# Down weights asked for in blocks of 64 partitions by four successive rows, with the hidden units renumbered to match

## The chip, the cores and the metric

The kernel runs on one core of a Trainium2 chip. The metric is the device time of one execution in microseconds (us). Before the change the median of three runs is 2054.45 us (2053.09 to 2056.13). The time of the changed kernel is compared with that.

## The reference, cut to what matters

The reference is a chain of two blocks of two layers each, in float32, on 256 tokens of width 1024. The change touches only the second layer of the first block: a mixture of 8 experts, of which each token uses 2. What is computed there is

```
def swiglu(x, w_gate_up, w_down):
    g, u = jnp.split(x @ w_gate_up, 2, axis=-1)
    return (jax.nn.silu(g) * u) @ w_down

out = sum over e of combine[:, e:e+1] * swiglu(xf, w_gate_up[e], w_down[e])
# w_gate_up[e]: 1024 x 7168 (gate 3584 columns, up 3584 columns);  w_down[e]: 3584 x 1024
```

Per expert that is 29.36 MB of gate and up weights and 14.68 MB of down weights, 352 MB for all eight, and each byte is read once from HBM. The hidden width of 3584 may be numbered in any order as long as gate, up and the rows of down agree.

## The kernel before

The kernel gathers for each expert at most 96 of its tokens (`CAPACITY`), as three groups of 32 (`TRIPLE`, `GROUP`), and runs the experts one after the other. If more tokens chose an expert, a second path (`r == "f"`) takes the rest; the change leaves it alone.

**Up and gate.** For the products with the gate weights (`EG`) and the up weights (`EU`) the 32 gathered tokens of a group are the stationary operand (128 rows of the contraction by 32 columns), and the weights stream past as the moving operand. TensorE's 128 columns are used as four quarters (`QUADS`): quarter z multiplies the same 32 tokens by another quarter of the weight columns and writes partitions 32z to 32z+31 of a PSUM bank. The 3584 hidden columns are done in two parts, `half` 0 of 2048 columns and `half` 1 of 1536. So one instruction has 512 moving columns in half 0 and 384 in half 1 (`UNITS_OF`). In the profile these are the groups of L1376; each float32 product stands there as two records.

Which weight columns quarter z takes is set in `up_tile` at line 1371: a row of 2048 weights is seen as (t z j) with j of 128, so quarter z takes four pieces of 128 columns (three in half 1), 512 columns apart.

**Turning.** The gate goes through SiLU on ScalarE and is multiplied by up on VectorE (L3124). The product `gated` has tokens on partitions; the down product needs hidden units there. VectorE turns it in blocks of 32 by 32 (`dve.transpose`, L3128). One block takes 32 columns of `gated` that lie 4 apart. After it, partition p and block (t, c) hold hidden unit 512t + 4p + c of the half.

**Down.** In `down`, 32 columns of the turned tensor are stationary and 256 columns of a down weight row are moving, again with four quarters (L1408). Tile k holds 512 rows of the down weights as 128 partitions by 4 rows; partition p has rows 4p to 4p+3 of the 512, which is what the turned order asks for.

**Loads.** All weights come through `ring`, five slots of 2 MiB. SyncE's instruction stream (SP) issues two transfers per tile (`load`, L924), each after waiting for the slot to be given back by TensorE (L921). `sources` says which bytes they take. For a gate or up tile each of the two takes 128 partitions by one row piece of 8 KB (half 0) or 6 KB (half 1). For a down tile the first takes rows 0 and 1 of each partition's four, and the second rows 2 and 3: 128 partitions by 8 KB each. TensorE waits for a whole tile (both transfers, a count of 32) in `weights`. The order of tiles per expert is: gate half 0 (4 tiles), up half 0 (4), gate half 1 (4), up half 1 (4), down (7). TensorE does them in that order.

The sequence of instructions around the change is written out by hand, and no planner decides anything here. Loads run ahead of TensorE by as much as the five slots allow.

Of the kernel before, what the change touches and what calls it, by code (L numbers as in the profile page):

```python
# [17 lines left out]
P = 128  # L18
SEQ, D = 256, 1024
TB = SEQ // P  # L20
KC = D // P
LAYERS = 2
EPS = 1e-6
WIDE = 512
# [9 lines left out]
D_FF, EXPERTS, D_EXP = 2816, 8, 3584  # L34
# [365 lines left out]
def kernel_program(nc, t):  # L400
# [30 lines left out]
    with ctx:  # L431
# [58 lines left out]
        def shaped(v, *shape):  # L490
            if len(shape) == 1:
                return v
            names = "abcd"[:len(shape)]
            return v.rearrange(f"p ({' '.join(names)}) -> p {' '.join(names)}",
                               **{k: s for k, s in zip(names[1:], shape[1:])})
# [357 lines left out]
        def tile_view(name, k, n):  # L853
            r = tiles_f if name in tiles_f.place else tiles
            return ring[:, r.slot(name), 0:k * n].rearrange("p (k n) -> p k n", n=n)

        def parts(src, k):

            v = src.rearrange("(k p) n -> p k n", p=P)
            return [(0, k // 2, v[:, 0:k // 2, :]), (k // 2, k, v[:, k // 2:k, :])]  # L860
# [35 lines left out]
        def sources(name, e):  # L896

            kind = name[0]
            if kind in ("EG", "EU") and name[1] == "m":
                a, n = HALF * name[2] + D_EXP * (kind == "EU"), QUADS * UNITS_OF[name[2]]  # L900
                rows = slice(name[3] * 2 * P, (name[3] + 1) * 2 * P)
                return 2, n, parts(t["moe_w_gate_up"][0, e, rows, a:a + n], 2)
            if kind in ("EG", "EU"):
                a = name[2] * WIDE + D_EXP * (kind == "EU")
                return KC, WIDE, parts(t["moe_w_gate_up"][0, e, :, a:a + WIDE], KC)
            down = t["moe_w_down"][0, e, name[2] * WIDE:(name[2] + 1) * WIDE, :]
            if name[1] == "m":
                down = down.rearrange("(p k) n -> p k n", k=4)
                return 4, D, [(0, 2, down[:, 0:2, :]), (2, 4, down[:, 2:4, :])]
            return 4, D, parts(down, 4)  # L910

        block = ctx.enter_context(nc.Block())

        @block.sync
        def _(sp):
            def load(name, what, i=None):
                r, fu, fe = ((tiles_f, f_tile_full, f_tile_free) if name in tiles_f.place
                             else (tiles, tile_full, tile_free))
                k, n, pieces = what
                sp.wait_ge(fe[r.slot(name)], r.freed(name, i))  # L920
                sp.sem_inc(asked, 1)  # L921
                v = tile_view(name, k, n)
                for a, b, src in pieces:
                    sp.dma_start(v[:, a:b, :], src).then_inc(fu[r.slot(name)], 16)  # L924

            def load_half(half):
                s = raws.slot(half)
                if raws.before(half) > 0:
                    sp.wait_ge(raw_free[s], raws.before(half))
                if in_two(half[0]):  # L930
                    for g in range(2):
                        sp.dma_start(raw_view(half)[:, :, g * 256:(g + 1) * 256],
                                     dense_source(*half, g)).then_inc(raw_full[s], 16)
                else:
                    sp.dma_start(raw_view(half), dense_source(*half)).then_inc(raw_full[s], 16)

            sp.dma_start(h[:, 0, :], t["x"][0, 0:P, :]).then_inc(x_in, 16)
            sp.dma_start(h[:, 1, :], t["x"][0, P:SEQ, :]).then_inc(x1_in_out_done, 16)
            first, first_from = raw_view(DENSE[0]), dense_source(*DENSE[0])
            sp.dma_start(flat(consts[:, 0:2, :]), t["common_constants"][:, 0:2 * P]).then_inc(ident_piece_in, 16)  # L940
            sp.dma_start(first[:, 0:2, :], first_from[:, 0:2, :]).then_inc(ident_piece_in, 16)
            sp.dma_start(first[:, 2:4, :], first_from[:, 2:4, :]).then_inc(raw_full[raws.slot(DENSE[0])], 16)
            for half in DENSE[1:FIRST_HALVES]:
                load_half(half)
            used = set()
            for name in expert_tiles("m"):
                slot = tiles.slot(name)
                if slot not in used:
                    used.add(slot)
                    for s in range(NRAW):  # L950
                        if RAW_AT[s] * HALF // TILE == slot:
                            sp.wait_ge(raw_free[s], sum(raws.slot(half) == s for half in DENSE[:FIRST_HALVES]))
                    for s in range(NTOP):
                        if TOP_AT[s] * HALF // TILE == slot:
                            sp.wait_ge(top_free[s],
                                       sum(tops.slot(half) == s for half in DENSE[:FIRST_HALVES] if half in tops.place))
                if slot == NSLOT - 1:
                    sp.wait_ge(*full(("RT",)))
                load(name, sources(name, 0), 0)
            with sp.Fori(1, EXPERTS) as e:  # L960
                for name in expert_tiles("m"):
                    load(name, sources(name, e), e)
            sp.wait_ge(flag_ready, 1)
            over_any = sp.value_load(flag_word)
            with sp.If(over_any > 0):
                for turn in range(ROUNDS_F // EXPERTS):
                    with sp.Fori(0, EXPERTS) as e:
                        for name in expert_tiles("f"):
                            load(name, sources(name, e), e + turn * EXPERTS)
                for s in range(NSLOT):  # L970
                    sp.wait_ge(f_tile_free[s], tiles_f.used[s] + F_CREDIT)
            for k, half in enumerate(DENSE[FIRST_HALVES:]):
                if k < NRAW:
                    s = RAW_AT[raws.slot(half)] * HALF // TILE
                    sp.wait_ge(tile_free[s], tiles.used[s] + F_CREDIT)
                load_half(half)
            pieces = [(0, 0, D), (1, 0, WIDE), (1, WIDE, D)]
            for k, (b, a, z) in enumerate(pieces):
                sp.wait_ge(h_new, LAYERS + 2 + k)
                sp.dma_start(t["out"][0, b * P:(b + 1) * P, a:z], h[:, b, a:z]).then_inc(x1_in_out_done, 16)  # L980
            sp.wait_ge(x1_in_out_done, 16 + 16 * len(pieces))
# [3 lines left out]
        def _(pe):  # L985
# [376 lines left out]
            def token_experts(meanwhile):  # L1362
# [5 lines left out]
                def up_tile(kind, half, k, e, o):  # L1368
                    name, u = (kind, "m", half, k), UNITS_OF[half]
                    weights(name, e)  # L1370
                    w = tile_view(name, 2, QUADS * u).rearrange("p q (t z j) -> p q z t j", z=QUADS, j=P)
                    for q in range(2):
                        c = 2 * k + q
                        for i in range(TRIPLE):
                            for z in range(QUADS):
                                mm = pe.matmul(shaped(o[i][GROUP * z:GROUP * (z + 1), 0:u], u // P, P),  # L1376
                                               xg[:, c, GROUP * i:GROUP * (i + 1)], w[:, q, z, :, :], start=c == 0,
                                               stop=c == KC - 1)
                            if c == KC - 1 and i < TRIPLE - 1:
                                mm.then_inc(*end((kind, "m", half, i)))  # L1380
                    mm.then_inc(*tile_end(name))
# [1191 lines left out]
        def _(dve):  # L2573
# [542 lines left out]
            def token_experts():  # L3116
                choose(0, sel_ready)

                def hidden(half, e):
                    for i in range(TRIPLE):  # L3120
                        dve.wait_ge(*drained(("EG", "m", half, i), e))
                        dve.wait_ge(*full(("EU", "m", half, i), e))
                        v = gated[half][:, i, :]
                        dve.tensor_tensor(v, v, out_of(("EU", "m", half, i))[:, 0:UNITS_OF[half]],  # L3124
                                          ALU.mult).then_inc(*fr(("EU", "m", half, i)))
                    for i in range(TRIPLE):
                        dve.wait_ge(*drained(("EU", "m", half, i), e))
                        dve.transpose(hidT_m[half][:, i, :].rearrange("p (t c g) -> p t c g", c=4, g=GROUP),  # L3128
                                      gated[half][:, i, :].rearrange("p (t f c) -> p t c f", c=4, f=GROUP)).then_inc(hidT_turned, 1)

                def expert(e, follows):
                    if follows:
# [516 lines left out]
```

## Time and profile before

| what | value |
|---|---|
| median of three runs | 2054.45 us |
| the profiled execution's own time | 2055.25 us |
| its span (first to last instruction) | 2053.5 us |
| around the span | 1.75 us |
| TensorE busy | 2038.2 us, 99% |
| VectorE busy, ScalarE busy | 901.2 us, 678.0 us |
| bytes moved by DMA | 570.78 MB |
| L1376 (gate and up products), TensorE busy | 580.4 us |
| L1408 (down products), TensorE busy | 295.0 us |

The eight experts take the stretch from 667 us to 1554 us of the span. A busy share of an engine says that an instruction was in flight on it, not that it ran at its peak; for L1376 and L1408 the mean time of one record therefore has to be held against its columns. Four quarters run at the same time, so a record's own duration (some 380 to 590 ns) is about four or more times what it costs. The cost is the group's busy time divided by its count.

### The profile page before, as it was taken

Reading aid. Unit: us, or ns where it says so; the run is one execution under the profiler, and the core shown is the slowest. Engines: PE = TensorE matmul, PEld = TensorE weight load, DVE = VectorE, ACT = ScalarE, POOL = GpSimd, SP = SyncE. Lnnn points to the kernel's source line nnn. Section 1 sums busy time; section 2 is a strip of 40 time slices with the busy share of each in tenths; the row PEclk is TensorE's granted clock in tenths of the full one; section 3 lists DMA queues with packets and bytes.
Section 4 is the critical chain, followed back from the end, with each engine's and each line's share of the span. In section 5 each row is a group of like instructions: output and inputs, shape, how many; then the busy total and the mean of one; then the engine's idle time right before and its main releaser. Section 6 shows DMA issues by size and latency. Waiting matters only on the chain.

```text
span 2053.5 us, 40234 instructions
## 1 busy us (share of the span) xinstructions
PE 2038.2 (99%) x17579; PEld 1362.0 (66%) x17579; DVE 901.2 (44%) x1251; ACT 678.0 (33%) x902; POOL 46.6 (2%) x69
## 2 busy tenths in 40 slices
PE   9999999999999999999999999999999999999998
PEld 6888888888888353434444353535357888888887
DVE  6777554467766100101010101010126878677775
ACT  5575543455755000000000000000005645556552
POOL 4100000000000000000000000000000000000000
PEclk9999999999999999999999999999999999999999
DMA  9654565554546999999999999999997544465442
GB/s 318 155 183 156 201 210 191 187 181 154 199 154 237 375 419 409 405 419 393 419 401 420 398 419 391 420 400 420 404 415 266 182 147 160 154 197 182 132 164 83
DMA packets 160046, 570.78 MB, mean 278 GB/s; under 512 B 13210, under 2 KB 26274, under 8 KB 128899
## 3 DMA queue, kind: packets, MB, share of 16 engines
q1 hardware_dynamic: 151040, 546.74, 70.8%
q0 software_dynamic: 5280, 17.16, 2.6%
q10 hardware_dynamic: 3554, 4.33, 0.6%
q8 instruction: 141, 2.31, 0.5%
q14 instruction: 31, 0.25, 0.0%
HBM read 562.80 MB, written 5.39 MB: 277 GB/s over the span
## 4 chain that ended last, share of the span: by engine, by line
PE 95%; DMA 4%; DVE 1%; ACT 0%; issue 0%; SPq 0%; DVEq 0%; POOL 0%; ACTq 0%; POOLq 0%
PE bank L1021 39%; PE bank L1376 25%; PE bank L1408 14%; PE bank L1076 5%; DMA ring<-moe_w_down 3%; PE bank L1094 2%; PE bank L1083 2%; PE bank L1027 1%; DMA ring<-w_in 1%; PE bank L1120 0%; PE bank L1633 0%; PE bank L1641 0%; PE bank L1640 0%; PE bank L1661 0%; PE bank L1647 0%; PE bank L1639 0%
## 5 line engine op out<-in xcount | busy, mean ns | idle before, releaser
L1021 PE MATMUL bank<-halves_r,x_both 128*128 128x512 f32 x2624 | 607.8, 390 | 0.0
L1376 PE MATMUL bank<-ring,xT 128*32 128x512 f32 (+1 forms) x6144 | 580.4, 539 | 0.0
L1021 PEld LDWEIGHTS bank<-halves_r,x_both 128*128 128x128 f32 x2624 | 489.9, 188 | 101.8 <-issue 1.5
L1376 PEld LDWEIGHTS bank<-ring,xT 128*32 128x32 f32 x6144 | 198.7, 110 | 373.0 <-issue 370.3
L2595 DVE TENSOR_TENSOR halves_r<-ring,halves_r 128x2048 fp32r<-128x2048 f32 x170 | 384.1, 2287 | 132.9 <-ACT halves_r L2021 131.3
L2021 ACT ACTIVATE halves_r<-ring 128x2048 fp32r<-128x2048 f32 x172 | 325.1, 1914 | 193.5 <-DMA ring<-w_in 78.0
L3124 DVE TENSOR_TENSOR arena<-arena,bank 128x512 f32<-128x512 f32 (+1 forms) x48 | 29.8, 620 | 726.7 <-PE bank L1376 725.3
L1408 PE MATMUL bank<-ring,arena 128*32 128x256 f32 x5376 | 295.0, 381 | 4.6 <-DMA ring<-moe_w_down 4.6
L1408 PEld LDWEIGHTS bank<-ring,arena 128*32 128x32 f32 x5376 | 181.8, 110 | 116.5 <-issue 11.7
L2208 ACT ACTIVATE arena<-bank 128x512 f32<-128x512 f32 (+1 forms) x58 | 32.1, 553 | 439.2 <-PE bank L1376 406.6
L1076 PE MATMUL bank<-x_both,halves_r 128*128 128x512 f32 x448 | 107.6, 392 | 0.6 <-DVE arena L2601 0.3
L1076 PEld LDWEIGHTS bank<-x_both,halves_r 128*128 128x128 f32 x448 | 82.4, 188 | 19.1 <-issue 1.6
L1021 PE MATMUL bank<-halves_r,yT_high 128*128 128x512 f32 x256 | 80.7, 392 | 0.0
L2289 ACT ACTIVATE arena<-bank 128x512 f32<-128x512 f32 (+1 forms) x14 | 6.1, 488 | 211.2 <-PE bank L1408 211.2
L2274 ACT ACTIVATE xT<-bank 128x512 f32<-128x512 f32 x16 | 8.8, 595 | 153.7 <-PE bank L1094 147.8
L1083 PEld LDWEIGHTS bank<-x_both,halves_r 128*128 128x128 f32 x448 | 57.4, 191 | 2.2
L1083 PE MATMUL bank<-x_both,halves_r 128*128 128x256 f32 x448 | 58.1, 283 | 0.0
L1021 PE MATMUL bank<-halves_r,hidT_high 128*128 128x512 f32 x176 | 55.0, 391 | 0.0
L1021 PEld LDWEIGHTS bank<-halves_r,yT_high 128*128 128x128 f32 x256 | 47.9, 188 | 9.8
L1999 ACT ACTIVATE arena<-bank 128x512 f32<-128x512 f32 x54 | 30.8, 596 | 61.6 <-PE bank L1021 50.5
L3128 DVE STREAM_TRANSPOSE arena<-arena 128x512 f32<-128x512 f32 (+1 forms) x48 | 45.5, 1001 | 0.0
L1094 PE MATMUL bank<-consts,arena 128*128 128x128 f32 x340 | 45.1, 274 | 0.0
(412 smaller groups left out, 1560.0 us busy)
## 6 DMA issues: line engine op xcount, KB each, us to landing
ring<-moe_w_gate_up SPq DMA_DIRECT2D x128, 1024.0 KB, 14.7
ring<-moe_w_down SPq DMA_DIRECT2D x112, 1024.0 KB, 13.0
ring<-w_in SPq DMA_DIRECT2D x99, 1024.0 KB, 5.2
ring<-moe_w_gate_up SPq DMA_DIRECT2D x128, 768.0 KB, 10.2
ring<-w_out SPq DMA_DIRECT2D x24, 1024.0 KB, 4.9
ring<-ffn_w_gate_up SPq DMA_DIRECT2D x20, 1024.0 KB, 5.2
ring<-ffn_w_down SPq DMA_DIRECT2D x11, 1024.0 KB, 5.0
ring<-w_in SPq DMA_DIRECT2D x18, 512.0 KB, 6.3
```

The lines of the kernel that those rows point to most:

```text
L1021: return pe.matmul(o[:, a:a + n], x[:, c, b * P:(b + 1) * P], w[:, k, col:col + n], **flags)
L1076: mm = pe.matmul(shaped(o[:, :], 2, SEQ), w[:, k, j * P:(j + 1) * P], x_pair[:, :, c, :], start=c == 0, stop=False)
L1083: mm = pe.matmul(o[:, 0:SEQ], w[:, k, j * P:(j + 1) * P], xT_high[:, c, :], start=False, stop=c == KC - 1)
L1094: mm = pe.transpose(o[:, k * P:(k + 1) * P], v, order)
L1376: mm = pe.matmul(shaped(o[i][GROUP * z:GROUP * (z + 1), 0:u], u // P, P), xg[:, c, GROUP * i:GROUP * (i + 1)], w[:, q, z, :, :], start=c == 0,
L1408: mm = pe.matmul(o[i // 2][GROUP * q:GROUP * (q + 1), Q_D * (i % 2):Q_D * (i % 2 + 1)], hidT_m[half][:, i, b:b + GROUP], w[:, c, Q_D * q:Q ...
L1999: act.activation(dst, src, func, scale=scale).then_inc(*fr(job))
L2021: act.activation(top_view(half), raw_view(half), ACT.Copy).then_inc(top_in, 1)
L2208: act.activation(dst, out_of(job)[:, 0:n], ACT.Silu).then_inc(*fr(job))
L2595: dve.tensor_tensor(raw_view(half, halves_r), raw_view(half), top_view(half).bitcast(F32), ALU.subtract).then_inc(raw_low_in, 1)
L3124: dve.tensor_tensor(v, v, out_of(("EU", "m", half, i))[:, 0:UNITS_OF[half]], ALU.mult).then_inc(*fr(("EU", "m", half, i)))
L3128: dve.transpose(hidT_m[half][:, i, :].rearrange("p (t c g) -> p t c g", c=4, g=GROUP), gated[half][:, i, :].rearrange("p (t f c) -> p t c ...
```

## The change

Three things change together, all inside the expert stage.

1. The columns that quarter z takes are one unbroken range: 512 z to 512 z + 511 in half 0 and 384 z to 384 z + 383 in half 1, where they were four (three) pieces of 128.
2. The block turned by VectorE takes 32 columns that lie 16 apart (12 in half 1), where they lay 4 apart. The output is written as before. Partition p and block t now hold hidden unit 16p + t (12p + t) of the half.
3. The down tile must follow: partition p of tile k takes the four rows 16p + 4k' to 16p + 4k' + 3 of the half (12p + ... in half 1), k' being the tile's number in the half. They are still four rows that follow one another in HBM, 16 KB; the next partition's rows start 64 KB (48 KB) further. The two transfers of the tile are cut otherwise: the first takes partitions 0 to 63 with all four rows, the second partitions 64 to 127. Each still moves 1 MB.

No instruction is added, removed or moved on any engine. The two DMAs of a down tile go from 128 partitions by 2048 elements to 64 partitions by 4096.

```diff
@@ sources
-            down = t["moe_w_down"][0, e, name[2] * WIDE:(name[2] + 1) * WIDE, :]
             if name[1] == "m":
-                down = down.rearrange("(p k) n -> p k n", k=4)
-                return 4, D, [(0, 2, down[:, 0:2, :]), (2, 4, down[:, 2:4, :])]
-            return 4, D, parts(down, 4)
+                half, k = divmod(4 * name[2], HALF // P)
+                down = t["moe_w_down"][0, e, half * HALF:min(D_EXP, (half + 1) * HALF), :]
+                down = down.rearrange("(p k) n -> p k n", p=P)
+                return 4, D, [(p, p + P // 2, down[p:p + P // 2, k:k + 4, :]) for p in (0, P // 2)]
+            return 4, D, parts(t["moe_w_down"][0, e, name[2] * WIDE:(name[2] + 1) * WIDE, :], 4)
@@ load
-                    sp.dma_start(v[:, a:b, :], src).then_inc(fu[r.slot(name)], 16)
+                    part = v[a:b] if name[:2] == ("ED", "m") else v[:, a:b, :]
+                    sp.dma_start(part, src).then_inc(fu[r.slot(name)], 16)
@@ up_tile
-                    w = tile_view(name, 2, QUADS * u).rearrange("p q (t z j) -> p q z t j", z=QUADS, j=P)
+                    w = tile_view(name, 2, QUADS * u)
...
-                                mm = pe.matmul(shaped(o[i][GROUP * z:GROUP * (z + 1), 0:u], u // P, P),
-                                               xg[:, c, GROUP * i:GROUP * (i + 1)], w[:, q, z, :, :], start=c == 0,
-                                               stop=c == KC - 1)
+                                mm = pe.matmul(o[i][GROUP * z:GROUP * (z + 1), 0:u], xg[:, c, GROUP * i:GROUP * (i + 1)],
+                                               w[:, q, u * z:u * (z + 1)], start=c == 0, stop=c == KC - 1)
@@ hidden
-                        dve.transpose(hidT_m[half][:, i, :].rearrange("p (t c g) -> p t c g", c=4, g=GROUP),
-                                      gated[half][:, i, :].rearrange("p (t f c) -> p t c f", c=4, f=GROUP)).then_inc(hidT_turned, 1)
+                        dve.transpose(hidT_m[half][:, i, :].rearrange("p (t g) -> p t g", g=GROUP),
+                                      gated[half][:, i, :].rearrange("p (f t) -> p t f", f=GROUP)).then_inc(hidT_turned, 1)
```

## Rows read from the trace of the kernel before

**Rows 1.** The page: TensorE's share, what DMA moved in 40 slices, the chain.
```profile
PE 2038.2 (99%) x17579; PEld 1362.0 (66%) x17579; DVE 901.2 (44%) x1251; ACT 678.0 (33%) x902; POOL 46.6 (2%) x69
...
GB/s 318 155 183 156 201 210 191 187 181 154 199 154 237 375 419 409 405 419 393 419 401 420 398 419 391 420 400 420 404 415 266 182 147 160 154 197 182 132 164 83
...
PE 95%; DMA 4%; DVE 1%; ACT 0%; issue 0%; SPq 0%; DVEq 0%; POOL 0%; ACTq 0%; POOLq 0%
```
**Rows 2.** Groups by line and form, 850 to 1760 us: busy us, mean ns | idle.
```profile
L1408 PE MATMUL bank<-ring,arena 128*32 128x256 f32 x4704 | 258.4, 381 | 4.6 <-DMA ring<-moe_w_down 4.6
L1376 PE MATMUL bank<-ring,xT 128*32 128x512 f32 x2304 | 248.3, 592 | 0.0
L1376 PE MATMUL bank<-ring,xT 128*32 128x384 f32 x2304 | 188.1, 486 | 0.0
...
L3128 DVE STREAM_TRANSPOSE arena<-arena 128x512 f32<-128x512 f32 x18 | 19.3, 1128 | 0.0
L3128 DVE STREAM_TRANSPOSE arena<-arena 128x384 f32<-128x384 f32 x21 | 17.3, 874 | 0.0
```
**Rows 3.** TensorE in order of time, 1100 to 1320 us: start, length, work.
```profile
1108.61 45.25 PE L1376 MATMUL bank<-ring,xT 128*32 128x512 f32 x432
...
1154.11 27.30 PE L1376 MATMUL bank<-ring,xT 128*32 128x384 f32 x336
1181.79 5.39 PE L1408 MATMUL bank<-ring,arena 128*32 128x256 f32 x96 [0.38 <-DMA ring<-moe_w_down]
1187.10 1.09 PE L1094 MATMUL bank<-consts,arena 128*128 128x128 f32 x8
1188.13 31.29 PE L1408 MATMUL bank<-ring,arena 128*32 128x256 f32 x576
1219.23 45.25 PE L1376 MATMUL bank<-ring,xT 128*32 128x512 f32 x432
```
**Rows 4.** TensorE's waits, 660 to 1560 us: us in total, times, longest.
```profile
PE bank L1408 <- DMA ring<-moe_w_down: 4.6, 4, 2.8
```
**Rows 5.** Stretches of one expert's cycle; the last row is the whole cycle.
```profile
1151.20:1161.20 10.00, 10.00 (x126) 4.00 (x122) 2.83 (x4) 0.00 (x0) 0.94 (x1) 1.00 0.95 350
...
1174.00:1208.00 34.00, 33.62 (x564) 19.22 (x560) 4.72 (x9) 1.09 (x2) 0.00 (x0) 1.00 1.01 419
1208.00:1247.00 39.00, 39.00 (x472) 15.21 (x468) 0.00 (x0) 3.95 (x6) 0.00 (x0) 1.00 1.01 420
1247.00:1261.80 14.80, 14.80 (x148) 4.63 (x144) 2.50 (x4) 0.00 (x0) 0.00 (x0) 1.00 0.97 389
1151.20:1261.80 110.60, 110.22 (x1458) 48.26 (x1454) 10.05 (x17) 6.50 (x11) 0.94 (x1) 1.00 1.00 409
```
**Rows 6.** DMA of that cycle: packets and MB; issues with us to landing.
```profile
DMA packets 7246, 45.24 MB, mean 409 GB/s; under 512 B 820, under 2 KB 1204, under 8 KB 3394
...
ring<-moe_w_gate_up SPq DMA_DIRECT2D x16, 1024.0 KB, 15.5
ring<-moe_w_down SPq DMA_DIRECT2D x14, 1024.0 KB, 12.9
ring<-moe_w_gate_up SPq DMA_DIRECT2D x16, 768.0 KB, 10.1
```
**Rows 7.** What SP waited for in that cycle: us, times, longest.
```profile
SPq L921 <- PE bank L1376: 55.9, 14, 9.2
SPq L921 <- PE bank L1408: 28.8, 7, 5.3
```
**Rows 8.** VectorE in order of time, 1150 to 1265 us: start, length.
```profile
1150.66 3.21 DVE L3128 STREAM_TRANSPOSE arena<-arena 128x512 f32<-128x512 f32 x3
...
1181.94 2.48 DVE L3128 STREAM_TRANSPOSE arena<-arena 128x384 f32<-128x384 f32 x3
```
**Rows 9.** Stretches of 5 us at the last expert's first down tile.
```profile
1510.00:1515.00 5.00, 3.19 (x40) 1.04 (x32) 2.78 (x5) 0.00 (x0) 0.00 (x0) 1.00 1.01 413
1515.00:1520.00 5.00, 3.98 (x44) 2.64 (x48) 1.13 (x2) 0.00 (x0) 0.00 (x0) 0.66 1.02 422
```

Columns of the rows of stretches (rows 5 and 9): stretch, length, busy us (and instructions) of PE, weight load, VectorE, ScalarE, GpSimd, then TensorE's granted clock as a share of full speed, the busy share of the 16 DMA engines, and GB/s.

## The prediction

> **What bounds the kernel now.** I read the page first [rows 1]. TensorE is busy for 2038.2 of 2053.5 us, so the whole kernel has 15.3 us in which it waits. DMA moves 83 to 318 GB/s outside the experts' stage, but in its 17 slices 375 to 420. That stage is the only one the change touches, and it has two candidates for its bound.
>
> Then I held TensorE's work against its columns [rows 2]. A record of 512 columns costs 248.3 us / 2304 = 107.8 ns, one of 384 costs 188.1 / 2304 = 81.6 ns, one of 256 costs 258.4 / 4704 = 54.9 ns. From 256 to 512 columns that is 52.9 ns more, 0.207 ns a column; carried back to no columns at all 2 ns are left. The groups are paced by their columns alone, so TensorE is at its rate here and its 99% is real.
>
> The timeline [rows 3] gives the cycle: half 0 starts at 1108.61 and again at 1219.23, 110.62 us. In it TensorE waits once, 0.38 us, at the first down tile. Over all experts it waits 4.6 us for down weights, in four waits, the longest 2.8 us [rows 4].
>
> Then DMA in the same cycle [rows 5, 6]. It moves 45.24 MB in 110.6 us, 409 GB/s, with a busy share of 1.00. Where the queue is full it moves 419 to 420. At 420 the cycle's bytes take 107.7 us. So the transfers have 2.9 us to spare per expert, 2.6%, and that is all. SP spends 84.7 us of the cycle waiting for slots [rows 7], and a 1 MB transfer lands 13 to 15 us after its issue [rows 6] though it needs only 2.5 us at 420 GB/s: five or six are queued. TensorE is the bound, and DMA stands right behind it. Anything that slows a third of the bytes by more than 2.9 us per expert makes DMA the bound.
>
> **Part 1: unbroken moving columns.** No instruction is added or removed. If pieces of 128 columns cost something, the 512 and 384 column records, which are read in pieces, would stand above the line of the 256 column record, which is read unbroken. They don't: 107.8 / 512 = 0.211 and 81.6 / 384 = 0.213 ns a column against 54.9 / 256 = 0.214. Value 0. Bounds: no loss, since the unbroken form is the simpler one and is the form already running in L1408; at best the part above 0.2083 ns a column (two cycles at the upper clock level, divided over the four quarters) goes, 1.1 ns of a 512 record and 1.6 ns of a 384 one, of each of which L1376 has 3072: 8 us.
>
> **Part 2: the turn with a longer step.** Per expert three turns of 1128 ns and three of 874 ns [rows 2]. The source is already read with a gap between elements. I bound the new step between no change and twice the time, 3.4 and 2.6 us more per expert on VectorE. What hides it: the turns of half 0 end at 1153.87 [rows 8], and the first down tile that reads them starts at 1181.79 [rows 3]. Those of half 1 end at 1184.42, and the fifth down tile, the first to read them, starts at 1188.13 + 3 x 31.29/6 = 1203.8. The covers are 28 and 19 us, and VectorE has nothing else in between but 0.65 us of small work. Value 0 at both bounds.
>
> **Part 3: the down transfers.** 14 transfers of 1 MB per expert, as many as before, issued at the same places. Two things change in each.
>
> The piece of HBM that follows without a break goes from 8 to 16 KB. In the stretch where down weights flow the rate is 419, in the one with 8 KB pieces of gate and up it is 420 [rows 5]; with 6 KB pieces it is 389 at a share of 0.97. Per unit of share that is 401 against 416: per engine 245 ns for 6 KB and 315 ns for 8 KB, hence 35 ns per KB and 36 ns fixed; 16 KB would run at 440. The gain on 35.0 us of down transfers (14.68 MB at 419) is at most 1.7 us of DMA time per expert. As TensorE is the bound, only its waits can come back: 0 to 4.6 us in all.
>
> The other thing is the destination. Each transfer now writes 64 partitions, where all 16 engines wrote 128. No row shows a large transfer to half of the partitions. The ends: if the engines set the pace, the rate stays 419 and the cost is 0. If what takes the data on the partition side sets it, half of the partitions take half, 210 GB/s. Both fit the rows, since with 128 partitions the two limits can't be told apart; that 419 and 420 come out for quite different strides in HBM says only that HBM is not the limit. The two transfers of a tile do not mend it: they stand one behind the other in the queue, every engine does its share of the first and then its share of the second, so all are on the same half at nearly the same time.
>
> I take the slow end with a small discount, 1.9 times the time: engines that are a few us apart in the queue overlap one half with the other now and then. The down transfers go from 35.0 to 66.5 us, 31.5 more; 2.9 us are absorbed by the room there is; 28.6 us per expert, times 8, is 229 us.
>
> The Trainium skill's page "SBUF — State Buffer", section "Door 1: The DMA port swizzle", says that partitions 0 to 63 reach only 8 of 16 ports and gives 196 GB/s for a 1 MiB transfer to them, against 328 for all 128. Its section "Can I just issue two DMAs to hit both halves?" says that two transfers to the two halves serialize. This trace has no such transfer, so no row here agrees or disagrees. By that 196 the down transfers would take an estimated 74.9 us and the change would cost 296 us.
>
> A row does tell what else a wait brings: where TensorE waited 2.8 us for down weights the granted clock of the next 5 us is 0.66 [rows 9], a stay at the lower level (1.2 GHz). With waits of some 4 us before each down tile (9.5 us of transfer against 5.2 of work) this will be seen again. It costs little, since TensorE then has time over: a down tile at the lower level takes 10.4 us, about the transfer's own 9.5.
>
> **Sum.** 2053.5 + 0 + 0 + 229 = 2282.5, with the 1.75 us around the span 2284. The profiled execution (2055.25) is 0.8 us above the median, so 2283.5.
>
> **Rivals.**
>
> *A. The engines set the pace (no contention).* Then the rate stays at 419 or rises, and TensorE's columns remain the bound: 2054, between 2050 and 2056. For it: an engine at a share of 1.01 moves 26 GB/s, whichever rows it reads, which looks like a limit of the engine itself. Against it: nothing in the trace, only that the figure would be the same if the limit lay behind the engine.
>
> *B. Faster.* It is A with TensorE's waits for down weights gone, 4.6 us, as 16 KB pieces land the first tile earlier: 2054.5 - 4.6 = 2049.9. It decides from 0.4 us per expert earlier on, and 1.7 us are at hand. With part 1's upper bound as well, 2042. Against it: the waits come at one tile per expert, and in the chain of waits 95% is TensorE's own work [rows 1].
>
> *C. Half contention.* Engines that share a way drift apart by half of a transfer and stay apart, as each is held up by other packets at other times. The factor is then 1.5: 52.5 us, 17.5 more, 14.6 after the room, 117 us in all, 2171.
>
> *D. The HBM side.* Partitions now start 64 or 48 KB apart. If that cost a tenth of the down rate, 3.9 us per expert less 2.9 of room, 8 us: 2062. Against it: gate and up rows lie 28 KB apart and run at 420.
>
> **Chances.** The forecast's mechanism, with factors from 1.5 to 2 (C is its low end), 0.60; its own range is 2171 to 2315. A 0.26, B 0.08, D and other small losses 0.06. This kernel's measurement can tell about 0.2%, 4 us, from no change: faster 0.09, same 0.26, slower 0.65. The likeliest case gives the time, 2283. The range has to reach A, so it is 2048 to 2315, and leaves out most of B and the factors above 2.
>
> **What the profile would show.** If I am right: the row of L1408 has over 150 us of idle before it, released by moe_w_down, where it had 4.6; the stretch of down transfers shows 200 to 240 GB/s at a DMA share near 1, as each packet takes longer; the stretches with gate and up alone stay at 420; the cycle is 139 us. The means per record of L1376 and L1408 stay at 107.8, 81.6 and 54.9 ns wherever the clock is full. The turns may take up to twice as long with nobody waiting. If down transfers run at 400 or more, the mechanism is wrong and A or B holds. If the rate halves but the time doesn't move, my 2.9 us of room are wrong. If gate and up records get cheaper, part 1 is wrong.

## The result and the profile after

The changed kernel takes 2328.03 us in the median of six runs (2326.2 to 2337.01), against 2054.43 us (2052.24 to 2056.13) of the kernel before: 1.1341 times as long, interval 1.1329 to 1.1353. The forecast was slower, 2283 us with a range up to 2315. The direction and the place were right, the size was too small by 45 us: 229 us of loss were forecast and 273.6 measured, 34.2 us per expert in place of 28.6.

The page of the changed kernel, with the rows that answer to [rows 1], and the granted clock of TensorE in tenths:

```profile
PE 2121.2 (91%) x17579; PEld 1383.9 (60%) x17579; DVE 897.1 (39%) x1251; ACT 677.8 (29%) x902; POOL 46.6 (2%) x69
...
PEclk9999999999999899998989989899898999999999
...
GB/s 292 170 183 181 207 183 184 180 158 211 163 336 298 250 400 242 359 307 264 404 234 374 298 285 371 221 369 301 270 404 225 252 181 143 166 169 183 145 163 91
...
PE 72%; DMA 26%; SPq 1%; issue 0%; DVE 0%; ACT 0%; DVEq 0%; POOL 0%; ACTq 0%; POOLq 0%
```

Outside the experts nothing moved. Inside, the rate swings between 400 and 221 GB/s where it was level, and 26% of the chain is DMA where 4% were. TensorE's waits, 660 to 1850 us (they answer to [rows 4]: us in total, times, longest), and its groups by form in the same stretch (they answer to [rows 2]):

```profile
PE bank L1409 <- DMA ring<-moe_w_down: 175.0, 55, 7.7
PE bank L1378 <- DMA ring<-moe_w_gate_up: 19.2, 13, 4.2
```
```profile
L1409 PE MATMUL bank<-ring,arena 128*32 128x256 f32 x5376 | 371.7, 443 | 175.0 <-DMA ring<-moe_w_down 175.0
L1378 PE MATMUL bank<-ring,xT 128*32 128x512 f32 x3072 | 331.7, 592 | 1.7 <-DMA ring<-moe_w_gate_up 1.7
L1378 PE MATMUL bank<-ring,xT 128*32 128x384 f32 x3072 | 256.1, 491 | 17.6 <-DMA ring<-moe_w_gate_up 17.6
```

TensorE waits 55 times for the 56 down tiles of the eight experts. A record of 512 columns costs 331.7 / 3072 = 108.0 ns, as before (107.8). The down record costs 69.1 ns where it cost 54.9: its work did not grow, the clock was lower for part of it. TensorE in order of time in one expert, one row per down tile (it answers to [rows 3], where six tiles stand in one row):

```profile
1188.27 5.39 PE L1409 MATMUL bank<-ring,arena 128*32 128x256 f32 x96
1197.25 5.39 PE L1409 MATMUL bank<-ring,arena 128*32 128x256 f32 x96 [3.60 <-DMA ring<-moe_w_down]
1206.34 8.29 PE L1409 MATMUL bank<-ring,arena 128*32 128x256 f32 x96 [3.71 <-DMA ring<-moe_w_down]
1216.02 5.39 PE L1409 MATMUL bank<-ring,arena 128*32 128x256 f32 x96 [1.39 <-DMA ring<-moe_w_down]
```

A tile starts every 9.0 to 9.7 us, where it was one in 5.2. The tile of 8.29 us ran partly at the lower clock level (1.2 GHz): it took 2.9 us more than its neighbours, and the wait behind it is 2.3 us shorter than theirs. The stretches of that expert (columns as in [rows 5], to which they answer: gate and up weights of half 1 in flight, down weights, down weights, gate and up weights of the next expert, the whole cycle):

```profile
1150.00:1160.00 10.00, 10.00 (x128) 4.03 (x124) 0.00 (x0) 1.47 (x3) 0.00 (x0) 1.00 1.02 413
1175.00:1205.00 30.00, 20.03 (x296) 11.24 (x296) 2.56 (x6) 1.09 (x2) 0.00 (x0) 0.89 1.01 232
1205.00:1230.00 25.00, 18.74 (x256) 10.28 (x260) 0.00 (x0) 0.00 (x0) 0.00 (x0) 0.80 1.00 225
1240.00:1265.00 25.00, 24.25 (x232) 7.35 (x228) 0.00 (x0) 3.69 (x6) 0.00 (x0) 1.00 1.02 421
1144.90:1286.40 141.50, 119.22 (x1455) 51.93 (x1454) 9.62 (x16) 6.50 (x11) 0.93 (x1) 0.94 1.01 319
```

In the down stretches the DMA engines are as busy as ever (1.01, 1.00) and move 225 to 232 GB/s in place of 419. They do not lack work; every packet takes about twice as long. This cycle is the shortest of the six whole ones: they take 141.5 to 147.7 us, 144.6 on average, where the cycles of the kernel before take 110.0 to 111.2. The transfers issued in that cycle (they answer to [rows 6]):

```profile
ring<-moe_w_gate_up SPq DMA_DIRECT2D x16, 1024.0 KB, 20.3
ring<-moe_w_down SPq DMA_DIRECT2D x14, 1024.0 KB, 30.5
```

A down transfer now lands 30.5 us after its issue, where it was 12.9.

### The profile page after: what moved, and what is told of

It is laid out like the page before. It is cut to its first block, busy times and chain, and to the rows that moved or that the text cites. A ratio compares the mean times of both kernels' runs of the same rounds, so it can differ in the third digit from the quotient of the medians.

```text
span 2325.6 us, 40234 instructions
## 1 busy us (share of the span) xinstructions
PE 2121.2 (91%) x17579; PEld 1383.9 (60%) x17579; DVE 897.1 (39%) x1251; ACT 677.8 (29%) x902; POOL 46.6 (2%) x69
## 4 chain that ended last, share of the span: by engine, by line
PE 72%; DMA 26%; SPq 1%; issue 0%; DVE 0%; ACT 0%; DVEq 0%; POOL 0%; ACTq 0%; POOLq 0%
PE bank L1023 35%; DMA ring<-moe_w_down 23%; PE bank L1378 18%; PE bank L1409 5%; PE bank L1078 4%; DMA ring<-moe_w_gate_up 3%; PE bank L1085 2%; PE bank L1096 2%; PE bank L1029 1%; SPq L926 1%; PE bank L1122 0%; PE bank L1634 0%; PE bank L1641 0%; PE bank L1642 0%; PE bank L1662 0%
## 5 line engine op out<-in xcount | busy, mean ns | idle before, releaser
L1409 PE MATMUL bank<-ring,arena 128*32 128x256 f32 x5376 | 371.7, 443 | 175.0 <-DMA ring<-moe_w_down 175.0
L1409 PEld LDWEIGHTS bank<-ring,arena 128*32 128x32 f32 x5376 | 201.5, 127 | 345.0 <-issue 146.2
L1096 PEld LDWEIGHTS bank<-consts,arena 128*128 128x128 f32 x340 | 38.9, 141 | 5.6 <-issue 2.9
```

What stands on the lines that cost most here:

```text
L1096: mm = pe.transpose(o[:, k * P:(k + 1) * P], v, order)
L1409: mm = pe.matmul(o[i // 2][GROUP * q:GROUP * (q + 1), Q_D * (i % 2):Q_D * (i % 2 + 1)], hidT_m[half][:, i, b:b + GROUP], w[:, c, Q_D * q:Q ...
```

## The experiments

Each is timed beside the kernel before on the same chip. The first three ask which part of the change costs, the next five which partitions are slow and which are not, and the last five where the missing 45 us are.

### Which part

**Rows cut again.** The changed kernel with the transfers of a down tile over all 128 partitions, two rows each:

```diff
-                return 4, D, [(p, p + P // 2, down[p:p + P // 2, k:k + 4, :]) for p in (0, P // 2)]
+                return 4, D, [(0, 2, down[:, k:k + 2, :]), (2, 4, down[:, k + 2:k + 4, :])]
```

> The changed kernel with its down tiles again cut into rows 0-1 and rows 2-3 on all 128 partitions (8 KB pieces); the unbroken up columns, the long-stepped turns and the 64/48 KB pitch in HBM stay. Theory P (the destination: a transfer to partitions 0-63 has half of the way into the memory): all of the loss was the cut, so 2054 within 5 us, down stretch at 420 GB/s. Rival H (the pitch of 64 KB between partitions in HBM slows the reads): the down stretch stays near 225 GB/s and the time near 2328. Rival T (the turns or the up columns hold something up): over 2070 with TensorE's waits not on moe_w_down.

Measured: 2053.03 us, 0.9998 of before (0.9988 to 1.0007). The unbroken up columns, the longer step and the pitch of 64 and 48 KB together cost and bring nothing that can be told.

**The cut alone.** The kernel before, with only the cut by partitions:

```diff
-                return 4, D, [(0, 2, down[:, 0:2, :]), (2, 4, down[:, 2:4, :])]
+                return 4, D, [(p, p + P // 2, down[p:p + P // 2, :, :]) for p in (0, P // 2)]
```

> The kernel before with only the cut of the down tiles changed: partitions 0-63 with four rows (16 KB pieces), then partitions 64-127; columns, turns and the 16 KB pitch as before. Theory P: the whole loss, 2328 within 6 us, down stretch at 220-230 GB/s. Rival H: no pitch, no loss, 2054, 420 GB/s.

Measured: 2325.88 us, 1.134 of before (1.1317 to 1.1363). The whole loss is in this one edit; its down weights flow at 219 GB/s from 1176 to 1206 us. The rival with the pitch falls: here the pitch is 16 KB as before.

**One transfer of 2 MB**, 128 partitions by 16 KB:

```diff
+                return 4, D, [(0, P, down[:, k:k + 4, :])]
...
+                if len(pieces) == 1:
+                    sp.sem_inc(fu[r.slot(name)], 16)
```

> The changed kernel with each down tile asked for in one transfer of 128 partitions by 16 KB (2 MB); the second count of 16 that TensorE waits for is given at issue. Theory P: 16 KB pieces as such are harmless and a little better than 8 KB: 425-435 GB/s in the down stretch, 2048 to 2055. If 16 KB pieces were what is slow (rival B16: long pieces are held up), it stays near 225 GB/s and 2328.

Measured: 2052.63 us, 0.9996 (0.9987 to 1.0005). The stretch from 1176 to 1206 us, in which down weights flow, of this kernel, and after it the same stretch of the kernel with rows cut again (8 KB pieces):

```profile
1176.00:1206.00 30.00, 29.23 (x500) 16.90 (x494) 4.60 (x9) 1.09 (x2) 0.00 (x0) 1.00 1.01 428
```
```profile
1176.00:1206.00 30.00, 29.24 (x504) 17.19 (x500) 4.60 (x9) 1.09 (x2) 0.00 (x0) 1.00 1.01 420
```

Pieces of 16 KB are not slow. They run at 428 against 420, 2% faster, and TensorE's waits for down weights go from 5.0 to 2.3 us, which is within the noise of the whole.

### Which partitions

**Even and odd.** Two transfers of 64 partitions again, but interleaved:

```diff
+                return 4, D, [(p, P, down[p:P:2, k:k + 4, :]) for p in (0, 1)]
...
+                    part = v[a:b:2] if name[:2] == ("ED", "m") else v[:, a:b, :]
```

> The changed kernel with the two transfers of a down tile taking the even and the odd partitions, still 64 partitions by 16 KB each. If only the number of partitions counts (64 take half of 128), it stays at 220-230 GB/s and 2328. If it counts which partitions they are, and the even ones reach every way into the memory with each engine having its own, 420-430 GB/s and 2054. If each engine takes four partitions next in order, engines that are four apart still meet on the same ways, but for half of their share only, so that a small lag parts them: 250-350 GB/s and 2120-2260. My guess is the last.

Measured: 2052.89 us, 0.9998 (0.9988 to 1.0007). My guess, the middle case, was wrong. The same stretch:

```profile
1176.00:1206.00 30.00, 29.27 (x504) 17.19 (x500) 4.61 (x9) 1.09 (x2) 0.00 (x0) 1.00 1.01 426
```

64 partitions by 16 KB run at full rate. So it is not the number of partitions, and not the size or number of the pieces: it is which partitions one transfer holds.

**Every fourth partition**, four transfers of 32 partitions:

```diff
+                return 4, D, [(p, P, down[p:P:4, k:k + 4, :]) for p in range(4)]
```

> The changed kernel with each down tile in four transfers of 32 partitions by 16 KB, transfer r taking partitions r, r+4, r+8 and so on. Theory W (what counts is that each engine writes into its own way: with every fourth partition, as with every second, each engine keeps the groups of four partitions it has in a transfer of all 128): full rate, 420-430 GB/s, 2054 within 5 us. Rival S (small numbers of partitions are slow as such and the even-odd cut escaped it by being just wide enough): 200-300 GB/s and over 2150.

TensorE waits here for the counts of all four transfers, 64 in place of 32. Measured: 2052.5 us, 0.9995 (0.9985 to 1.0004), and 426 GB/s in the same stretch. A quarter of the partitions is enough for the full rate, if they are spread.

**The middle first.**

```diff
+                return 4, D, [(p, z, down[p:z, k:k + 4, :]) for p, z in ((P // 4, 3 * P // 4), (0, P // 4), (3 * P // 4, P))]
```

> The changed kernel with a down tile in three transfers of unbroken partitions: 32 to 95 (1 MB), 0 to 31 and 96 to 127 (512 KB each). If any unbroken range of 64 partitions is slow: 220-230 GB/s and 2328 or more. If it counts whether a transfer lies on one side of partition 64 (each side having its own eight ways): the first has both sides and runs at 420 or more, the two others are halved, so a tile takes 2.5 + 4.7 us: the down stretch of 14.68 MB takes 50 us in place of 35, near 290 GB/s, and the time is 2054 + 8 x 15 to 8 x 18 = 2174 to 2200.

Measured: 2316.95 us, 1.1281 (1.1246 to 1.1316), and from 1165 to 1220 us 231 GB/s. Neither reading fits: the first transfer should have been fast. By itself the run is inconclusive, since two of the three transfers lie on one side of partition 64 and may slow the third. So the two kinds were run alone.

**Only the middle** and **only the low half** of each down tile, the other 1 MB left out (the second count of 16 is given at issue):

```diff
+                return 4, D, [(32, 32 + P // 2, down[32:32 + P // 2, k:k + 4, :])]   # e11
+                return 4, D, [(0, 0 + P // 2, down[0:0 + P // 2, k:k + 4, :])]       # e12
```

> The changed kernel where only partitions 32 to 95 of each down tile are loaded (1 MB of its 2 MB; the other half of the products' weights is left out). Read is the rate while 16 KB pieces flow. Rival G (it counts which groups of partitions a transfer reaches: 32 to 95 reach as many as 128 do, so it is not slow): 420. Theory W (it counts who writes where; two neighbouring engines share a group of four here as in 0 to 63): 200-240.

> The changed kernel where only partitions 0 to 63 of each down tile are loaded (1 MB of its 2 MB; the other half is left out). Both W and G: 200-240 GB/s while these flow, as in the changed kernel. If instead the halving came from the two halves standing close behind each other in the queue, the low half alone would run faster than 300.

Measured: 2048.69 us for the middle and 2123.41 for the low half, one run each. Two stretches of the middle kernel in which, but for a few packets, only these transfers flow, then one of the low half:

```profile
1064.30:1067.30 3.00, 3.00 (x44) 1.19 (x39) 0.00 (x0) 0.00 (x0) 0.00 (x0) 1.00 1.01 431
1085.30:1088.30 3.00, 3.00 (x64) 1.80 (x58) 0.00 (x0) 0.00 (x0) 0.00 (x0) 1.00 1.00 426
```
```profile
1091.70:1109.70 18.00, 14.78 (x212) 7.33 (x212) 4.59 (x9) 1.09 (x2) 0.00 (x0) 0.91 1.00 207
```

Partitions 32 to 95, half on either side of 64, run at 426 to 431. Partitions 0 to 63 run at 207, also with no other half behind them. That is a little slower than the two halves in turn, which run at 216 to 227 GB/s through the slow stretches of the changed kernel, where the low half alone runs at 199 to 205 over the like stretches of its cycles. Theory W, which I had formed after the even and odd run, falls; G holds. It agrees with the rule of the Trainium skill, page "SBUF — State Buffer", section "Door 1: The DMA port swizzle": 0 to 63 reach 8 of the 16 ports, while by its table 32 to 95 (and the even ones) reach all. What these runs test of that rule is the side of partition 64 alone. The page's advice in the summary, to use 128 partitions, is stricter than these runs: 64 or 32 spread ones did as well.

### Where the other 45 us are

**Less work for TensorE**, in the kernel before and in the changed one, by the same edit:

```diff
-                        for i in range(TRIPLE):
+                        for i in range(TRIPLE if n in (0, EX_CH - 1) else TRIPLE - 1):
```

> The kernel before, where the third group of tokens is left out of 26 of the 28 row blocks of every down product: TensorE has 11 us less work per expert, and DMA the same. Theory R (DMA could do the cycle in 107.7 us): the cycle falls from 110.6 to about 107.7, 2031. Rival N (no room: down transfers take 35 us at their own pace, and the up tiles of half 1 stay at TensorE's pace): the cycle stays within 1 us of 110.6, 2046 to 2054.

> The changed kernel, where the third group of tokens is left out of 26 of the 28 row blocks of every down product, so that TensorE has 11 us less work per expert and a down tile at the lower clock level takes under 7 us, less than its transfer. Theory D (the 34 us more per expert are all transfers: 31 at half rate and the rest neighbours slowed at the edges): the cycle stays within 2 us of 144.6, so 2310 to 2330 with the last expert's own saving. Rival C (TensorE's stays at the lower clock delay the slots and cost 3 us or more per expert): 2290 or less.

Measured: 2041.57 us (0.9949, 0.9932 to 0.9965) and 2321.45 us (1.1313, 1.129 to 1.1336). A cycle of the first (the whole of it, columns as above), then TensorE's waits in the second:

```profile
1138.00:1246.90 108.90, 100.63 (x1247) 41.58 (x1243) 10.08 (x16) 6.50 (x11) 0.94 (x1) 1.00 1.01 414
```
```profile
PE bank L1409 <- DMA ring<-moe_w_down: 237.4, 56, 7.4
```

The kernel before, with TensorE out of the way, has a cycle of 108.9 us instead of 110.6, so transfers have 1.7 us to spare, not 2.9; neither expectation has it. The other cycles agree, 108.4 to 109.2 us. The share of the DMA engines is 1.01 in that cycle and the rate 414 GB/s, so 420 is not what a whole cycle can do. The changed kernel gains only 6.6 us in all from 11 us less TensorE work per expert; most of what TensorE saves it waits (237.4 in place of 175.0 us). So the lower clock, which makes some down tiles longer, is not where the 45 us are.

**One, three and two adjacent down tiles** cut into halves of the partitions, the others by rows. The condition is `name[2] == 3`, `name[2] in (1, 3, 5)` and `name[2] in (3, 4)`:

```diff
+                if not (name[2] == 3):
+                    return 4, D, [(0, 2, down[:, k:k + 2, :]), (2, 4, down[:, k + 2:k + 4, :])]
```

> The changed kernel where only one of the seven down tiles of an expert (the fourth) is cut into partitions 0-63 and 64-127; the others are cut by rows. At 222 GB/s that tile takes 9.4 us of transfer in place of 5.0. Theory R (the prediction's: 2.9 us of room per expert absorb the first part of a loss): 8 x (4.4 - 2.9) = 12 us, 2066. Rival N (there is no room: the stretches below 420 GB/s in the up tiles of half 1 are paced by TensorE giving slots back, and stay): 8 x 4.4 = 35 us, 2089. A tile cut alone whose delay hides behind what had landed ahead of it would give nothing, 2054.

> As before with one tile, but three of the seven down tiles (second, fourth, sixth) cut into halves of the partitions. Theory R: 8 x (13.2 - 2.9) = 82 us, 2136. Rival N: 8 x 13.2 = 106 us, 2160.

Measured: 2125.09 us (1.0342, 1.0311 to 1.0373) and 2258.1 us (1.0983, 1.0945 to 1.1022). Both are far above both expectations: 71.3 and 204.4 us over before, per expert 8.9 and 25.5, so 8.5 to 8.9 for a single tile, where all seven cost 34.2. The kernel with one such tile, in the 8 us before it, the 16 us around it and the 8 us behind it:

```profile
1095.60:1103.60 8.00, 7.56 (x125) 4.62 (x116) 3.96 (x6) 0.00 (x0) 0.00 (x0) 1.00 1.02 424
1103.60:1119.60 16.00, 11.23 (x197) 6.32 (x195) 0.65 (x3) 1.09 (x2) 0.00 (x0) 0.97 1.01 223
1119.60:1127.60 8.00, 6.42 (x84) 3.23 (x88) 0.00 (x0) 0.00 (x0) 0.00 (x0) 0.64 1.00 411
```

The tile is 2.1 MB, which at 223 GB/s is 9.4 us. But the rate is low for 16 us, in which 3.6 MB pass (14 to 17 us in the six cycles). The other 1.5 MB belong to transfers before and behind it, over all 128 partitions, and they are halved too: in the records of the single packets, one of 8 KB takes 313 ns between 1098 and 1103 us and 645 ns between 1115 and 1119 (medians). So a run of one-sided transfers costs its own bytes and an edge. With a per tile, b per unbroken run of tiles and r for room that absorbs a loss, all per expert: a + b - r = 8.9, 3a + 3b - r = 25.5, 7a + b - r = 34.2. From these a = 4.2, b = 4.1 and r = -0.6 us. The intervals of the runs leave a within 0.2 us, but r within 1.3 and b within 0.7: the 2.9 us of room are excluded, and no sign is seen of the 1.7. The difference b - r, 4.7 us, doesn't need the run with three tiles; how it divides does. Three numbers made from three runs always fit them, so the fit alone shows nothing. They were then put to the test with two adjacent tiles:

> The changed kernel where two down tiles that follow each other (the fourth and fifth) are cut into halves of the partitions, the others by rows. Per expert one such tile alone cost 8.9 us, three apart from each other 25.5, all seven in a row 34.2. Theory B (each tile costs 4.2 us for its own bytes, and each unbroken run of such tiles 4.1 us more at its edges, where other transfers are slowed with it; no room absorbs any): 2 x 4.2 + 4.1 + 0.6 = 13.1 us per expert, 105 in all, 2159. Rival L (a tile costs 8.9 us wherever it stands, and in the full change something else caps the loss): 17.8 us per expert, 2196.

Measured: 2154.63 us (1.0493, 1.0465 to 1.0521), 100.8 us over before, 12.6 per expert. That is 13.1 as expected within the interval of 0.7 us; a cost of 8.9 per tile wherever it stands (17.8) falls.

The changed kernel's own trace gives the same loss without the fit. Its first slow stretch and the one behind it, up to the next slow one:

```profile
730.00:804.00 74.00, 51.34 (x696) 26.22 (x688) 4.51 (x9) 1.09 (x2) 0.00 (x0) 0.86 1.01 218
804.00:876.50 72.50, 71.31 (x766) 25.75 (x770) 5.04 (x7) 5.42 (x9) 0.96 (x1) 0.98 1.00 402
```

The slow stretches of its six whole cycles take 71.3 us on average at 222 GB/s, so 15.8 MB pass in them, 1.1 MB more than the down weights. At 419 GB/s they would take 37.8 us. The 33.5 us between are nearly all of the 34.1 by which a cycle is longer; the 14.68 MB of down weights have 31 of them and the neighbours' bytes 2.4. So the two ways agree in the sum and not in how it divides: 29.4 us for the down bytes by the fit, 31 by the rates. Between the slow stretches the rate is 382 to 409 GB/s, no higher than the 409 of a whole cycle before: there no time is won back.

## Why the prediction was right and where it failed

**What bounds.** Right that TensorE was the bound and DMA stood close behind; right that a slower third of the bytes would make DMA the bound. The chain and the waits show it. The cycle was forecast as 139 us and is 144.6.

**Part 1, unbroken columns: 0.** Right: 108.0 against 107.8 ns for 512 columns, and with the rows cut again 107.8 and the whole time the same.

**Part 2, the turns: 0.** Right in time, but my bounds reached the wrong way: the turns became cheaper. From 850 to 1760 us, in the kernel with the rows cut again (they answer to the last two of [rows 2]):

```profile
L3129 DVE STREAM_TRANSPOSE arena<-arena 128x512 f32<-128x512 f32 x18 | 17.4, 1024 | 0.0
L3129 DVE STREAM_TRANSPOSE arena<-arena 128x384 f32<-128x384 f32 x21 | 16.6, 838 | 0.0
```

That is 1024 for 1128 ns and 838 for 874. Nobody waits for them.

**Part 3, the longer piece.** Right that it is worth nothing here; 440 GB/s was too high, 428 was measured.

**Part 3, the destination.** The mechanism was right: half of the way into the memory, 1.9 times the time, forecast as 66.5 us (221 GB/s) for the down bytes. Measured are 216 to 227 over its slow stretches, and 29.4 (by the fit) to 31 us more (by the rates) where I had 31.5. The 1.9 was a guess that came out. For its reason, that engines drifting apart overlap one half with the other, there is one sign, which is no proof: the low half alone, with no other half to overlap with, runs at 199 to 205, a little under half of 420.

**The step that failed** is "2.9 us are absorbed by the room there is", and with it the size of the loss per expert, "28.6 us". It had two errors of one sign. First, no room was absorbed that the runs could show. The 2.9 us came from comparing the mean rate of the cycle with 420. A whole cycle can do 414, which leaves 1.7. And what lies below 420 lies for the most part in the stretches with the 6 KB pieces [rows 5]; there TensorE gives slots back at its own pace, and in the changed kernel the rate between the slow stretches is no higher. That a loss in the down transfers can't shorten those stretches is my reading of it; the fit's r of -0.6 within 1.3 us is what was measured. Second, a term was missing: the edge of each run, 4.1 us per expert by the fit and 2.4 by the rates, in which transfers of gate and up weights are slowed that the change never touched. The sum becomes 29.4 + 4.1 + 0.6 = 34.1 per expert, 273 us; it meets the measured loss because that loss is one of the three numbers in the fit, and the two adjacent tiles are its test. With the room alone put right, 31.5 x 8 = 252 us and 2307 would have stood there, still 21 us short, and factor 2 would have given 35.0 x 8 = 280 us and 2334: the range ended at 2315 because of the same 2.9 us.

**Rivals.** A and B, with 0.34 of the chance, fall: the engines don't set the pace of a transfer to one side. For partitions 32 to 95, of the same size, A would have been right (426 to 431). C falls: an easing by drift, if there was one, was from about 203 to 222 GB/s and not to factor 1.5. D falls, the pitch costs nothing. The stay at the lower clock was right in kind and cost at most the 6.6 us that came back with less TensorE work.

What is not settled is how the engines share out the partitions of a transfer, and so how the edge comes about. That engines still busy with a one-sided transfer get in the way of those already at the next one is the first thing to think of, but it doesn't account for all: between 1116 and 1119 us of the kernel with one such tile 60 of the 65 weight packets that start are of 8 KB, from transfers over all 128 partitions, only two to four one-sided packets are in flight, and still the others take twice their time. No row here names the engine of a packet. Nor is it shown why the middle first kernel ran at 231 in all its down stretch (207 to 231 over five cycles); the same spill is the likely reason.

## What to carry to other kernels

A load that is cut into several transfers should be cut so that each has as many partitions below 64 as above, as in the cuts that ran at full rate here: by rows, even and odd, or every fourth; not into 0 to 63 and 64 to 127. Before a slack is set against a loss, find the stretch in which it lies and ask whether the loss is in that stretch. And a slow transfer must be priced with its neighbours in the queue: one 2 MB tile in a stream cost twice what its own bytes lose (8.9 against 4.2 us).

## What the runs showed of the hardware that was not expected

- A transfer of 32 partitions, four apart, runs at the full 426 GB/s, and 64 in the middle at 426 to 431; 64 in the low half at 207 (the last two from one run each).
- One 2 MB tile of one-sided transfers halves the rate of the whole core for 16 us, 3.6 MB, while the share of busy DMA engines stays at 1.01. Packets of other transfers take 645 ns in place of 313 in it.
- The block turn on VectorE in its new form took less time: 1024 against 1128 ns for 512 columns (elements 16 apart, they were 4 apart), 838 against 874 for 384 (12 apart). The new form also walks one dimension less; which of the two counts was not tested.
- Pieces of 16 KB give 428 GB/s where 8 KB give 420.
